# Hybrid decoder layer on one core: the input projection's load requests re-sorted, and four slabs of the last modulation gate multiplied around the end of sample attention

## What is computed

```python
mod = silu(c) @ w_ada + b_ada                     # w_ada: 2048 x 12288
shift1, scale1, gate1, shift2, scale2, gate2 = split(mod, 6)
h  = rmsnorm(x, norm1_g) * (1 + scale1) + shift1
qa, ka, va, qb, kb, vb, r, glr = split(h @ w_in)  # w_in: 2048 x 6160
oa = dilated attention (prompt; samples against a cache of 1024 rows)
ob = gated linear attention (GLA), 4 heads
x  = x + gate1 * (concat(norm(oa), norm(ob) * silu(r)) @ w_out)
h2 = rmsnorm(x, norm2_g) * (1 + scale2) + shift2
g_pre, u = split(h2 @ w_up)                       # w_up: 2048 x 11264
x  = x + gate2 * ((silu(conv(g_pre)) * u) @ w_down)
```

## Time and profile before

| | us |
|---|---|
| median of 3 runs | 1807.35 |
| lowest, highest | 1805.87, 1808.92 |
| the profiled execution, its time | 1814.6 |
| the profiled execution, its span | 1813.0 |
| PE busy in the span | 1714.2 |
| mean granted TensorE clock, share of full | 0.959 |

### The profile page before, as it was taken

How to read it: one execution, slowest core, us unless ns; L and a number is a source line. 1 busy time by engine, 2 the same in 40 slices (tenths; PEclk the granted TensorE clock), 3 DMA queues, 4 the chain that set the end, 5 groups by cost and what they waited for, 6 DMA issues and landing times.

```text
span 1813.0 us, 29118 instructions
## 1 busy us (share of the span) xinstructions
PE 1714.2 (95%) x12190; PEld 1515.0 (84%) x12190; DVE 864.7 (48%) x1458; ACT 714.8 (39%) x1000; POOL 77.0 (4%) x134
## 2 busy tenths in 40 slices
PE   5869999899999989989989999999999999999997
PEld 2328878688887885559978999999999999999997
DVE  1224343433455564345564545554555456566563
ACT  1212432433444553344353333333434345455452
POOL 2000000000110110000000000000000000000000
PEclk9859988989999999989999999999999999999999
DMA  9996565756676768868477455545454545555551
GB/s 329 299 367 216 189 225 179 246 187 218 228 243 209 237 225 320 317 206 295 149 261 250 148 179 165 164 143 186 159 168 143 187 151 160 160 177 171 177 165 35
DMA packets 284127, 373.17 MB, mean 206 GB/s; under 512 B 7985, under 2 KB 209043, under 8 KB 283577
## 3 DMA queue, kind: packets, MB, share of 16 engines
q1 hardware_dynamic: 276304, 350.93, 58.3%
q0 software_dynamic: 7680, 20.36, 3.2%
q10 hardware_dynamic: 18, 0.07, 0.0%
HBM read 361.45 MB, written 11.97 MB: 206 GB/s over the span
## 4 chain that ended last, share of the span: by engine, by line
PE 83%; DMA 8%; DVE 4%; ACT 2%; issue 2%; SPq 1%; POOL 0%; DVEq 0%; ACTq 0%; POOLq 0%
PE ps L831 22%; PE ps L832 21%; PE ps L833 21%; PE ps L778 4%; DMA ring<-in_w_ada 4%; DMA ring<-in_w_in 4%; PE ps L1070 2%; PE ps L1055 1%; PE ps L926 1%; PE ps L1108 1%; PE ps L972 1%; PE ps L785 1%; PE ps L745 1%; DVE wlo L1641 1%; DMA vals<-in_cache_v_win 1%
## 5 line engine op out<-in xcount | busy, mean ns | idle before, releaser
L831 PE MATMUL ps<-hhi,whi 128*128 128x288 f32 x3136 | 950.3, 303 | 6.4 <-DVE hlo L1747 2.8
L833 PE MATMUL ps<-hhi,wlo 128*128 128x288 f32 x3136 | 932.6, 297 | 0.0
L832 PE MATMUL ps<-hlo,whi 128*128 128x288 f32 x3136 | 932.5, 297 | 0.0
L831 PEld LDWEIGHTS ps<-hhi,whi 128*128 128x128 f32 x3136 | 597.7, 191 | 39.5 <-issue 28.3
L832 PEld LDWEIGHTS ps<-hlo,whi 128*128 128x128 f32 x3136 | 596.9, 190 | 1.3
L833 PEld LDWEIGHTS ps<-hhi,wlo 128*128 128x128 f32 x3136 | 596.8, 190 | 0.0
L1634 DVE TENSOR_TENSOR wlo<-ring,whi 128x1024 fp32r<-128x1024 f32 x178 | 212.3, 1222 | 94.0 <-ACT whi L1299 93.5
L1641 DVE TENSOR_TENSOR wlo<-ring,whi 128x1024 fp32r<-128x1024 f32 x128 | 155.5, 1222 | 201.0 <-ACT whi L1307 200.5
L1299 ACT ACTIVATE whi<-ring 128x1024 fp32r<-128x1024 f32 x178 | 184.7, 1058 | 163.6 <-PE ps L833 163.6
L1307 ACT ACTIVATE whi<-ring 128x1024 fp32r<-128x1024 f32 x128 | 133.3, 1054 | 157.5 <-DMA ring<-in_w_in 86.5
L778 PE MATMUL ps<-ring,c 128*32 128x512 f32 x656 | 106.0, 730 | 40.1 <-DMA ring<-in_w_ada 33.3
(11 more groups left out here) (279 smaller groups left out, 1214.7 us busy)
## 6 DMA issues: line engine op xcount, KB each, us to landing
ring<-in_w_up SPq DMA_DIRECT2D x88, 1024.0 KB, 5.2
ring<-in_w_ada SPq DMA_DIRECT2D x82, 1024.0 KB, 5.4
ring<-in_w_in SPq DMA_DIRECT2D x48, 1024.0 KB, 7.8
ring<-in_w_down SPq DMA_DIRECT2D x32, 1408.0 KB, 6.5
ring<-in_cache_k_win SPq DMA_DIRECT2D x16, 1024.0 KB, 8.4
vals<-in_cache_v_win SPq DMA_DIRECT2D x16, 1024.0 KB, 10.0
ring<-in_w_out SPq DMA_DIRECT2D x16, 1024.0 KB, 5.4
proj<-in_w_ada SPq DMA_DIRECT2D x14, 1024.0 KB, 9.1
```

Of the source, the lines that this page charges most:

```text
L831: mm(out, w_hi, x_hi, start=start, stop=False)
L832: mm(out, w_hi, x_lo, start=False, stop=False)
L833: return mm(out, w_lo, x_hi, start=False, stop=stop)
```

## The change

Two parts.

1. The keys of `order`: 2w-6 instead of 2w-4 for `in_half(w)`, `LATE_AT[m-2] + 1` instead of `LATE_AT[m-2]` for `in_late(m)`. No wait is changed, only which request stands behind which.
2. The gate slabs. A function `gate_home(q)` gives each slab its place: 0, 1 and 6 to 15 in `gate_rows`, 2 to 5 in ring slots 1 and 3. `gate_load(0)` and `gate_load(1)` are requested directly behind the last `value_loads`, 2 and 3 behind `out_half(1)`. PE multiplies slabs 0 and 1 between the last `other_keys` and the last `probabilities`, and 2 and 3 behind the last `output`. Six slabs remain at the end of the output projection (4 to 9) and six in the up projection (10 to 15, in its first turn). `late_rows(12)`, `late_turn(12)` and `late_mod(12)` move into the output projection, the others one place forward.

```diff
-        ODD_LESS = 7 * 16
+        ODD_LESS = 6 * 16
@@ gate_home
+        def gate_home(q):
+
+            if 2 <= q < 6:
+                return False, 1 + 2 * (q % 2), SL_OUT // SLOTS * 16 + (q // 2) * 16
+            l = q + 1 if q < 2 else (q - 6) % 4
+            return True, l, 16 if q < 2 else 16 * ((q - 6) // 4 + (2 if l in (1, 2) else 1))
@@ gate_load
-                if q < 2:
-                    sp.dma_start(slab(2 * q + 1, 4, 512), src).then_inc(full[2 * q + 1], 16)
+                spare, at, _ = gate_home(q)
+                if spare:
+                    if q >= 10:
+                        sp.wait_ge(raw_used, RAW_OUT + q - 3)
+                    sp.dma_start(gate_rows[:, at], src).then_inc(gate_in[at], 16)
                 else:
-                    if q >= 6:
-                        sp.wait_ge(raw_used, RAW_OUT + q - 3)
-                    sp.dma_start(gate_rows[:, (q - 2) % 4], src).then_inc(gate_in[(q - 2) % 4], 16)
+                    if q >= 4:
+                        sp.wait_ge(raw_used, RAW_OUT + q - 1)
+                    sp.dma_start(slab(at, 4, 512), src).then_inc(full[at], 16)
@@ SP, input projection
-            order = [(2 * w - 4, 1, w) for w in range(2, 48)] + [(LATE_AT[m - 2] if m >= 2 else m - 2, 0, m) for m in range(48)]
+            order = [(2 * w - 6, 1, w) for w in range(2, 48)]
+            order += [(LATE_AT[m - 2] + 1 if m >= 2 else m - 8, 0, m) for m in range(48)]
@@ SP, end of sample attention
             value_loads(NB // 2 - 1)
+            gate_load(0)
+            gate_load(1)
             sp.wait_ge(*ST.upto("k15", 3))
             out_half(0)
             out_half(1)
+            gate_load(2)
+            gate_load(3)
@@ PE, sample attention
                 if g < NB // 2 - 1:
                     first_keys(g + 1)
+                else:
+                    gate_slab(0)
+                    gate_slab(1)
                 probabilities(g)
             values(NB // 2 - 1)
             output(NB // 2 - 1)
+            gate_slab(2)
+            gate_slab(3)
@@ PE, output projection
+                if m == 7:
+                    late_turn(12)
@@
-            for q in range(3):
+            for q in range(4, 7):
                 gate_slab(q)
             norm2_sum(7)
-            for q in range(3, 6):
+            for q in range(7, 10):
                 gate_slab(q)
-            late_turn(12)
@@ PE, up projection, behind a unit
-                    if c == 3 and i * 4 + u < 5:
-                        gate_slab(6 + 2 * (4 * i + u))
-                        gate_slab(7 + 2 * (4 * i + u))
+                    if i == 0 and c == 3:
+                        if u != 2:
+                            late_turn((13, 14, None, 15)[u])
+                        if u < 3:
+                            gate_slab(10 + 2 * u)
+                            gate_slab(11 + 2 * u)
@@ ACT, behind the two squares at the start of the output projection
+            late_rows(12)
```

More of the change, by code:

```diff
@@ L578, in _ @@
                 if w < 12:
-                    gate_load(w - 6)
+                    gate_load(w - 2)
                 out_half(w)
@@ L585, in _ @@
             for s in (1, 3):
-                sp.wait_ge(raw_used, RAW_OUT + 1 + s // 2)
+                sp.wait_ge(raw_used, RAW_OUT + 5 + s // 2)
                 half_load(w_up, s, columns[s // 2], s)
-            for q in range(6, 10):
+            for q in range(10, 14):
                 gate_load(q)
             half_loads(w_up, columns, CH_UP, range(4, 7))
[L591 to L598, removed]
             gate_load(14)
             gate_load(15)
-            half_loads(w_up, columns, CH_UP + 16, range(3, 8))
+            half_loads(w_up, columns, CH_UP, range(7, 8))
+            half_loads(w_up, [512, D_FF + 512, 768, D_FF + 768], CH_UP + 16)
             with sp.Fori(2, 11) as i:
@@ L845, in gate_slab @@
             def gate_slab(q):
-                if q == 4:
-                    pe.wait_ge(*BV.upto(*late("mod", 11)))
-                if q in (8, 12):
+                if q in (0, 4):
                     pe.wait_ge(*BS.upto(*late("rows", 11 + q // 4)))
[L851 to L857, removed]
+                if q == 12:
+                    pe.wait_ge(*BS.upto(*late("rows", 14)))
+                spare, at, landed = gate_home(q)
+                pe.wait_ge(gate_in[at] if spare else full[at], landed)
+                ada_slab((3, 5, 7, 7)[q // 4], q, gate_rows[:, at] if spare else slab(at, 4, 512))
             def late_turn(G):
@@ L1162, in _ @@
             for m in range(32):
+                if m == 2:
+                    pe.wait_ge(*BS.upto(*late("rows", 12)))
                 out_product(m)
@@ L1313, in late_rows @@
                 act.wait_ge(*BT.upto(*late("turn", G - 1)))
-                f(mrow[:, :], ps[:, 3 if G < 12 else 5 if G == 12 else 7, :], ACT.Copy).then_inc(*BS.step(f"rows{G % 2}"))
+                f(mrow[:, :], ps[:, 3 if G <= 12 else 5 if G == 13 else 7, :], ACT.Copy).then_inc(*BS.step(f"rows{G % 2}"))
             def spent(i, chunks, j):
@@ L1502, in _ @@
             norm_root(1)
-            late_rows(12)
+            late_rows(13)
             for j in range(2):
@@ L1536, in up_turn @@
                 his(6, 8)
-                if i < 2:
-                    late_rows(13 if i == 0 else 15)
+                if i == 0:
+                    late_rows(14)
                 silu(0)
@@ L1543, in up_turn @@
                 if i == 0:
-                    late_rows(14)
+                    late_rows(15)
                 silu(1)
@@ L2096, in _ @@
                     norm2_scaled(n)
+                if j == 13:
+                    late_mod(12)
             norm_mean(1, 4)
@@ L2112, in _ @@
             norm2_lo(3, 3)
-            late_mod(12)
             dve.wait_ge(*UV.upto("u3", 1))
@@ L2165, in up_turn @@
                 los(6, 10)
+                if i == 0:
+                    late_mod(13)
                 gate(0)
                 los(10, 14)
-                if i < 2:
-                    late_mod(13 if i == 0 else 15)
+                if i == 0:
+                    late_mod(14)
                 conv(1)
@@ L2182, in up_turn @@
                 if i == 0:
-                    late_mod(14)
+                    late_mod(15)
             for i in range(11):
```

## The result

| | before | after |
|---|---|---|
| median of the comparison, us | 1806.61 (4 runs) | 1786.16 (4 runs) |
| lowest, highest | 1803.98, 1808.92 | 1781.82, 1790.73 |
| ratio, with its 95% interval | | 0.9888 (0.9856 to 0.9919) |
| the profiled execution, its time | 1814.6 | 1788.47 |

The change makes the kernel 20.4 us faster; 13.3 was forecast. A later comparison of the same kernel gave less, as will be seen.

The account below looks back on a forecast made before the run. The kernel was taken as PE-bound (busy 1714.2 of 1813.0 us), reducible through PE's idle time and lower-clock time. Request order -18 us plus gate slabs +4.7 gave -13.3, from 1807.35 to 1794.0 us; range 1786.5 to 1804.

Parts of the forecast that it names:

- Part 1, the idle time: Input projection: earlier requests for `w_in` halves remove PE's idle time behind late loads, 11.5 us plus perhaps 1.
- The three places: PE's idle times in the input projection: 3.16 us before 261.56, 5.94 before 353.97, 3.29 before 546.54; gain 11.5 us.
- several waits under 1 us: Input projection: PE's small waits for tile copies behind late splits, said to add perhaps 1 us of gain.
- Part 1, the clock: Input projection: PE's lower clock around its three idle times goes with them, 5.9 us gained together.
- Part 2, the hole: End of sample attention: PE waits for slabs 0 and 1, which land behind the values; `probabilities` begins 10.2 us later.
- an earlier issue doesn't help: End of sample attention: issuing slabs 0 and 1 earlier gains nothing, since the queue is full with values.
- Part 2, what comes back: After the wait for slabs: 0.8 us from `values`, 2.0 from `head_sums(0)`, 2.7 net from slabs leaving the up projection.
- the bound of part 1, -22: Input projection: largest gain of the request order, 22 us, if all small waits go and one GLA stretch shortens.
- Half a gain in part 1: Input projection: ACT or DVE reach the next dependence just as late, so only 8 us gained; 1804.0, chance 0.13.
- slower: Request order gains under 5 us in the input projection, slabs cost 7.6 at sample attention's end; 1812, chance 0.07.
- More: Input projection gains 22 us or more as a GLA stretch shortens, moved slabs cost only 2.7; 1788, chance 0.12.
- The slabs fill the gap: End of sample attention: slabs land by 783.5, ahead of the values, giving -4.7 us there; 1784.6, chance 0.02.

Follow-up runs that it names:

- e1: The kernel before with only the new request-order keys, no slab moved; median 1782.65 us, ratio 0.9898.
- e2: The changed kernel with the old request-order keys, so only the gate slabs are moved; median 1811.97 us, ratio 1.0030.
- g1: The kernel before with the new request order only where the GLA heads run (up to chunk 50), no slab moved; 1791.07 us, ratio 0.9923.
- w1: The kernel before with five unused matmuls behind the first slab of the first half of w_ada; median 1806.13 us, ratio 0.9994.
- h1: The kernel before with seven unused matmuls behind the first w_ada slab and one each behind the second and third; 1807.35 us, ratio 1.0000.
- e3: The changed kernel with gate slabs 0 and 1 requested ahead of the last values instead of behind them; median 1776.49 us, ratio 0.9843.
- e4: The changed kernel measured once more, unchanged, beside the other experiments; median 1790.90 us, ratio 0.9921.
- w3: The changed kernel with the same five unused matmuls as w1; median 1789.25 us, ratio 0.9898.
- w2: The kernel before with the new request order and the same five unused matmuls as w1, no slab moved; median 1783.09 us, ratio 0.9872.
- h2_hot_ahead: The kernel of e3 with the unused matmuls of h1; 1778.30 us, ratio 0.9850.

## Why the prediction was right and wrong

**What bounds the kernel.** Right: idle time of PE behind loads and the clock that fell with it. The idle time shrank where the order was changed and nowhere else (`e1`, `e2`, `g1`). By windows of 1 us, all four traces of the old order (before, `e2`, `w1`, `h1`) have 3.4 us at the lower clock at the first place and 6.8 at the second; the nine with the new order there have neither.

**Part 1, the idle time.** The three places went as forecast. They fell from 12.4 to 0.3 us, 12.1 gained for 11.5. The step that failed is the enumeration: the three places were taken for nearly all of the idle time, and "several waits under 1 us" were priced at "perhaps 1"; they gave 4.5 in the profile pair (16.6 - 12.1). The row that would have warned is the windows' first one of the kernel before, 539.70 us with 516.16 busy: 23.5 us idle, of which the three places are 12.4 and the rest, 11.1, was never added up. It bounds the term and doesn't size it: of the 11.1, 6.6 stayed. Over the traces of the old order (before, `e2`, `w1`, `h1`) the idle time is 23.0 to 24.9, over those of the new one 6.9 or 7.0: 17 us against the forecast 12.5. Besides the three, five waits for ACT's tile copies went from 2.3 to 0.3, six for DVE's softmax from 7.6 to 2.6, where the third place had only 3.3 of it, and two waits for DVE at L946, 1.0 us in all, went.

**Part 1, the clock.** 5.9 us were forecast for the three places. PE's busy time gives nearly that: 4.0 us less in the two windows from stretch to stretch (56.82 + 59.84 against 56.00 + 56.67, with 823 and 824 matmuls) and 1.8 less in the part with the pairs, where the third place lies (197.59 against 195.80), 5.8 in all. In the profile pair the whole stage was busy 10.1 us less. The other 4.3 lie elsewhere in the GLA part, for which the forecast had nothing: the second of the four GLA stretches was 10.2 us at the lower clock instead of 13.7, and the first products had 3.7 us of it instead of 6.6 (windows of 1 us). Whether the change did that is open. The second stretch has 13.7 us in three of the four traces of the old order and 6.8 in `w1`; with the new one it has 10.2 in eight of nine and 6.8 in `e1`. But the four stretches together, 38 to 51 us and 41 to 48, overlap. Over the traces PE was busy 509.6 to 516.2 us with the old order and 503.2 to 506.8 with the new (`g1` left out), 8 between the means.

Both terms together are 25 us between the means of the traces (538.1 from 534.3 to 539.7, against 512.7 from 510.1 to 513.7), 7 more than the 18 forecast and outside its bounds of 8 and 22: the idle time left out gave 5 of them, busy time outside the three places the other 2.

**Part 2, the hole.** Right to a few tenths where it was worked out from landings: slabs 2.7 us apart (2.9 forecast), 8.2 and 0.7 us of waiting (some 9 and some 1), the values 8.9 us later (about 10). That "an earlier issue doesn't help" was right only for places behind the values: ahead of them (`e3`) the hole went. That the Trainium skill ("DMA: Bandwidth & Descriptors", "Queues, rings and completion order") has each DMA engine consume a ring's descriptors in order, agrees: slab and values landed in the order of issue, and turning that order round moved the hole.

**Part 2, what comes back.** The values were to gain 0.8 from two slabs ahead of them; they took 6.66 us against 5.91, so 0.7 was lost instead: PE had stood 8 us before those slabs, and they ran at the lower clock too (1.93 and 1.94 us). `head_sums(0)` came down to 2.18 as forecast (2.0 back). Behind them 5.8 us came back in the two last stages (4.5 + 1.3) for the forecast 4.7 of slabs and `head_sums` together. The 3.7 us by which the up projection alone was to be shorter didn't show as such: PE was busy 4.3 us less and the stage 1.3 shorter, since 3.0 us of idle time came in for `hlo`. In all +9.6 - 4.5 - 1.3 = +3.8 in the profile pair, +4.7 forecast. Behind the start, the traces give +4.6 (`e2` against before), +5.5 (`e4` against `e1`) and +3.6 (`w3` against `w2`).

**The sum.** By medians part 1 was -23.5 (`e1`) and -23.0 (`w2` against `w1`) where -18 was forecast; part 2 was +5.9 (`e2`), +6.2 (`w3` against `w2`) and +8.2 (`e4` against `e1`) where +4.7 was. The ratios give less: -18.4 and -22.0 for part 1, +5.4, +4.7 and +4.2 for part 2, with intervals of some 6 us to either side for `e1` and `w2`. So the times alone would not show that part 1 was sized too small; the traces do, by 7 us, and they put part 2 within 1.1 of its forecast. All of the miss lies in the first. The range failed at its lower end because the bound of part 1, -22, was made of the small waits and one GLA stretch as mishaps in a rival of 0.12, where the stage's idle time made the small waits a likely case. How large the gain of the whole is, the runs don't settle: the changed kernel came out 20.4 us faster in one comparison and 15.2 in another (0.9888 and 0.9921, intervals that overlap); the second would be 1793 from 1807.35, next to the forecast. Nor do stages and times agree fully: in the traces of the change all that lies behind the start is 22.9 and 23.2 us shorter, and the medians show 20 and 15; for `g1` it is 19.1 against 13. Single runs of one kernel spread over 9 to 18 us, of which the start alone can make 11; that is more than what is left, so this stays open.

**Rivals.** Half a gain in part 1, and slower: refuted by `e1`. More: its size came about (1788 against 1786), but not for its reason; part 2 was not at its lower bound, and of the two causes named for part 1 it was first the small waits, while a shorter GLA stretch gave some 1.7 us in the profile pair (half of 13.7 - 10.2), with its cause open. The slabs fill the gap: not in this order of requests; with the slabs ahead of the values (`e3`) exactly that happens, at 6 us below the order alone.

## What to carry to other kernels

Before the single waits are priced, subtract the busy time from the length of the stage: what the places you can name don't cover needs a price or a reason to stay, and one cause can stand behind many small waits, which go with it. When work is moved into a gap of an engine, ask where its data stand in the queue: two slabs behind 5 MB of values cost 9.6 us, ahead of them they were free, with not one instruction more. In one issuing queue, order requests by the time at which their slot becomes free, then look at the waits of the engine that unpacks them.

## What the hardware showed that was not expected

When the clock rises in the start differs from execution to execution of the same instructions. With the same instructions and PE busy 24 of 25 us the slabs took 1.94 us each until 29 us in one trace and until 56 in others, and the part ahead of the input projection 124 to 136 us. The Trainium skill ("TensorE: Matmul & The Clock Gate", "Part 1: The HAM clock gate") has it that activity releases the throttle; here the idle matmuls gave that activity, and the clock was up at about 20 us and down again by 23 in one trace (`w1_warm_before`), up from 20 to 67 in another (`h2_hot_ahead`). That agrees only in part: without idle matmuls PE was busy 24.2 of 25 us in a slow start and 23.7 in a quick one, and yet the clock rose up to 27 us later in one trace than in another. No run shows what decides it.

The stretches at 0.50 of the GLA heads, where PE is busy throughout, come in different lengths for the same instructions. Windows of 15 us over the second of them, in the kernel before and in `w1_warm_before`, with the same order of requests:

```profile
293.50:308.50 15.00, 15.00 (x62) 13.36 (x65) 2.79 (x5) 1.66 (x3) 0.00 (x0) 0.54 0.07 21
```

```profile
290.50:305.50 15.00, 15.00 (x77) 12.24 (x77) 5.31 (x10) 4.48 (x6) 0.57 (x1) 0.77 0.22 72
```

A mean clock of 0.54 over 15 us is 13.8 us at the lower level (1.2 GHz), one of 0.77 is 6.9. Two of the four stretches of `w1_warm_before` are that short, 13.7 us less at the lower clock than in the kernel before, which accounts for the 6.6 us by which its PE was busy less in the input projection (509.6 against 516.2).
